# Where a streamed product turns its sums: three edits to a two-network transformer kernel

## The reference, cut to what matters

```
m = silu(c) @ mod_w + mod_b                       # both conditions, both layers
x = x + 0.5 * g0 * ffn1(norm(x) * (1 + sc0) + sh0)   # d_ff 2816, silu gated
x = x + g1 * mixer(norm(x) * (1 + sc1) + sh1)
x = x + 0.5 * g2 * ffn2(norm(x) * (1 + sc2) + sh2)
# first mixer: [latent attention, 8 heads | conv of width 31, then layer norm over 512 channels, silu] @ w_out
# second transformer: partial rope by cos/sin of positions * freq on 16 of 64 dimensions
```

## Time and profile before

| | |
|---|---|
| median of three runs | 3402.97 us |
| the profiled execution's own time | 3398.24 us |
| its span, first to last instruction | 3396.5 us |
| granted TensorE clock, mean | 0.976 |
| TensorE busy | 95% |
| weight loads of TensorE busy | 84% |
| VectorE busy | 60% |
| ScalarE busy | 42% |
| HBM read over the span | 140 GB/s |

### The profile page before, as it was taken

One profiled execution on the slowest core, in us unless ns is written; L12 is line 12 of the kernel. 1 busy time (PEld: TensorE's weight loads), 2 busy tenths in 40 slices (PEclk: granted clock), 3 DMA queues, 4 the chain that ended last, 5 costly groups with the idle time before them and its releaser, 6 DMA issues. The chain is left out here.

```text
span 3396.5 us, 51226 instructions
## 1 busy us (share of the span) xinstructions
PE 3223.1 (95%) x20294; PEld 2865.6 (84%) x20294; DVE 2026.9 (60%) x2665; ACT 1428.2 (42%) x2342; POOL 181.8 (5%) x151
## 2 busy tenths in 40 slices
PE   5999999889999999999889999999999999999998
PEld 4878777468787788877579999899999999999998
DVE  4776759747777633335445566556466665654665
ACT  3333334633333322224454444445454544454543
POOL 1000011000000100020000000300000002100000
PEclk8999999989999999999999999999999999999999
DMA  7566632026666333332136656553556665543664
GB/s 226 156 180 180 172 95 78 13 69 177 176 188 183 101 87 108 88 101 87 50 86 170 178 165 181 157 173 100 148 160 187 177 185 153 166 132 109 177 180 130
DMA packets 769421, 478.28 MB, mean 141 GB/s; under 512 B 37973, under 2 KB 746165, under 8 KB 769093
## 3 DMA queue, kind: packets, MB, share of 16 engines
q1 hardware_dynamic: 767200, 474.88, 49.3%
q10 hardware_dynamic: 2020, 0.64, 0.1%
HBM read 474.40 MB, written 1.05 MB: 140 GB/s over the span
## 5 line engine op out<-in xcount | busy, mean ns | idle before, releaser
L537 PE MATMUL psum<-normed,weights_part 128*128 128x256 f32 (+1 forms) x7392 | 1311.0, 338 | 32.0 <-DVE normed L867 11.6
L537 PEld LDWEIGHTS psum<-normed,weights_part 128*128 128x128 f32 x7392 | 1140.7, 192 | 186.9 <-issue 35.7
L523 DVE TENSOR_TENSOR weights_part<-weights,weights_part 128x2048 fp32r<-128x2048 f32 (+1 forms) x413 | 884.9, 2143 | 365.1 <-ACT weights_part L515 364.8
L515 ACT ACTIVATE weights_part<-weights 128x2048 fp32r<-128x2048 f32 (+1 forms) x413 | 739.1, 1792 | 811.1 <-PE psum L537 418.7
L537 PE MATMUL psum<-hidden,weights_part 128*128 128x256 f32 (+1 forms) x4224 | 680.4, 323 | 0.0
L537 PEld LDWEIGHTS psum<-hidden,weights_part 128*128 128x128 f32 x4224 | 614.5, 191 | 61.2
L537 PE MATMUL psum<-unscaled,weights_part 128*128 128x256 f32 x4224 | 515.3, 285 | 8.9 <-DVE unscaled L675 6.8
L537 PEld LDWEIGHTS psum<-unscaled,weights_part 128*128 128x128 f32 x4224 | 511.2, 193 | 11.4 <-DVE unscaled L675 8.6
L1086 DVE SCALAR_TENSOR_TENSOR stage<-weights,cond,stage 128x768 f32<-128x768 f32 x294 | 281.0, 1018 | 0.0
L406 POOL TENSOR_TENSOR square<-square,rinvs 128x256 f32<-128x256 f32 (+1 forms) x39 | 57.2, 1467 | 2773.6 <-ACT rinvs L391 2772.1
L880 DVE TENSOR_TENSOR rinvs<-rinvs,psum 128x256 f32<-128x256 f32 (+1 forms) x88 | 45.8, 520 | 163.2 <-ACT rinvs L774 163.2
(11 more groups left out here) (445 smaller groups left out, 2650.6 us busy)
## 6 DMA issues: line engine op xcount, KB each, us to landing
weights<-in_l_ffn_w_in SPq DMA_DIRECT2D x176, 512.0 KB, 5.1
weights<-in_ffn_w_gu SPq DMA_DIRECT2D x176, 512.0 KB, 5.0
weights<-in_l_mod_w SPq DMA_DIRECT2D x168, 384.0 KB, 3.4
weights<-in_w_in SPq DMA_DIRECT2D x34, 1024.0 KB, 5.2
weights<-in_w_gate SPq DMA_DIRECT2D x64, 512.0 KB, 5.2
weights<-in_l_ffn_w_out SPq DMA_DIRECT2D x64, 384.0 KB, 4.1
weights<-in_ffn_w_down SPq DMA_DIRECT2D x64, 384.0 KB, 3.9
weights<-in_l_ffn_w_out SPq DMA_DIRECT2D x64, 320.0 KB, 3.3
```

The costliest lines, as they stand in the source:

```text
L515: k.nc.scalar.activation(k.parts[part][0][:, W], k.slots[slot][:, W], ACT.Copy).then_inc(k.high_done, 1)
L523: k.nc.vector.tensor_tensor(k.parts[part][1][:, W], k.slots[slot][:, W], k.parts[part][0][:, W].bitcast(F32), ALU.subtract).then_inc(k.spl ...
L537: mm = k.nc.tensor.matmul(to, left[a], right[b], start=first and n == 0, stop=last and n == len(PASSES) - 1)
```

## The change

Three parts. (1) `ModStream.turn` is called inside unit u: in a wide unit between its two tiles, in a narrow one between the fifth and sixth of its eleven chunks. (2) The rope tables become a class whose load stays where it was, while the angles and the sines come after the fifth wide unit (`BETWEEN`); the loops of VectorE and ScalarE over the eleven units are so cut into five and six, which `each_unit` writes out straight. (3) In the first mixer the reciprocal is done in four pieces of 128 columns in slots 23 to 26, the scaling goes to slots 29 to 32, and silu to slots 33 and 34 (two chunks each). Only one output unit is split early, in halves: high at s=25 and 26, low at s=27 and 28; the second is left to `add_product_of_parts`, which splits what isn't `ready` behind its eight chunks of `mixed_part`.

```
                     for tile, kc in tiles:
                         if first_unit and tile == 0:
                             pe.wait_ge(t["normed"].sem, t["normed"].base + kc + 1)
+                        if stream is not None and (tile, kc) == (1, 0):
+                            stream.turn(pe, at(spec, c))
                         mm = product_of_parts(...)
                     mm.then_inc(k.unit_done, 1)
-                    if stream is not None:
-                        stream.turn(pe, at(spec, c))
...
                     for kc in range(KH):
+                        if stream is not None and kc == KH // 2:
+                            stream.turn(pe, at(spec, c))
                         mm = product_of_parts(...)
                     mm.then_inc(k.unit_done, 1)
-                    if stream is not None:
-                        stream.turn(pe, at(spec, c))
...
-            between(act)
+            if between is not None:
+                between.load(act)
...
-                each_unit(act, 0, spec.n, unit_in if s % 2 == 0 else unit_out, looped(s))
+                begun = 0
+                if s == 0 and between is not None:
+                    each_unit(act, 0, BETWEEN, unit_in, looped(s))
+                    between.tables(act)
+                    begun = BETWEEN
+                each_unit(act, begun, spec.n, unit_in if s % 2 == 0 else unit_out, looped(s))
# the same on VectorE, with between.angles(dve)
...
-CONV_MEAN, CONV_VARIANCE, CONV_SCALED = 17, 22, 23
-HEAD_AHEAD = {28: 0, 31: 1}
+CONV_MEAN, CONV_VARIANCE, CONV_ROOT, CONV_SCALED = 17, 22, 23, 28
+OUT_HIGH, OUT_LOW = (25, 26), (27, 28)
...
-    k.ahead[out.name] = 2
+    k.ahead[out.name] = 1
...
+                if s in OUT_HIGH:
+                    half = out_halves[OUT_HIGH.index(s)]
+                    last = nc.scalar.activation(out_part[0][:, half], out_slot[:, half], ACT.Copy)
...
-                    for c in ((0,), (1, 2), (3,), (), ())[s - N_HEAD_JOBS]:
+                    for c in ((), (0, 1), (2, 3), (), ())[s - N_HEAD_JOBS]:
...
+                if s in OUT_LOW:
+                    half = out_halves[OUT_LOW.index(s)]
+                    last = nc.vector.tensor_tensor(out_part[1][:, half], out_slot[:, half], out_part[0][:, half].bitcast(F32), ALU.subtract)
...
-                if s == CONV_SCALED:
+                if CONV_ROOT <= s < CONV_ROOT + 4:
+                    piece = conv_inverse[:, (s - CONV_ROOT) * P:(s - CONV_ROOT + 1) * P]
                     dve.wait_ge(t["conv_root"].sem, t["conv_root"].base + 1)
-                    nc.vector.reciprocal(conv_inverse, conv_inverse).then_inc(t["conv_inverse"].sem, 1)
+                    nc.vector.reciprocal(piece, piece).then_inc(t["conv_inverse"].sem, 1)
```

## The result

The changed kernel takes 3498.3 us in the median of four runs (3492.8 to 3505.1), the kernel before 3403.3 (3398.1 to 3403.9). The ratio is 1.0284, with a 95% interval of 1.0258 to 1.0309. The forecast was 3481 with a range of 3450 to 3520. The profiled execution of the changed kernel took 3493.37 us, its span is 3491.6, which is 95.1 more than before.

What follows compares the result with a forecast made beforehand. TensorE, busy 95% of the span, was taken as the bound. Turns +77, clock +15, tables -1 and mixer -11 gave +80 on 3398.2, so 3478; the forecast was set at 3481, range 3450 to 3520 us.

Steps and rivals of the forecast that it cites:

- The mechanism of part 1: Streamed feed-forwards: each moved turn still waits for the same VectorE accumulations, now mid-unit; new waits sum to 99 us.
- 6.3 + 1.9n - 5.5: TensorE's wait in a wide unit, n being the place of the group's last step in its hook: 2.7, 4.6, 6.4 us.
- The old 22.3 us: TensorE's 11 existing waits ahead of turns, contained in the new 99 us and not paid twice: +77 us.
- The clock: TensorE runs slower after long idle stretches: ten of thirteen waits followed by a slow stretch of 1.5 us each, +15 us.
- VectorE's waits for the turn would fall under 10 us: Streams: VectorE's next group waits for the turn 12 times, 34.1 us in all, and that mostly goes.
- Part 2: Feed-forward with the tables: the 2.8 us wait ahead of TensorE's fourth unit goes, a later one comes; net -1 us.
- wait 2.2: Tables' feed-forward: ninth unit's low part ready at 1810.8, TensorE wants it at 1808.6, so it waits 2.2 us.
- Part 3: First mixer: three TensorE waits shrink to 0.8 us left of the first, -8.5; with 2.5 of slow matmuls, -11 us.
- The long fall of the clock: Rival: the clock falls for long after most waits, +60 us for the clock, 3523 us in all; chance 0.07.
- VectorE's catching up: Rival: VectorE, no longer held by turns, ends later accumulations earlier, up to 34 us off the new waits; 3437, chance 0.06.
- the free middle: Rival: accumulations are done by mid-unit, so turns cost TensorE nothing and the 22.3 us go; 3364 us, chance 0.04.
- The sum: Whole kernel: +77 + 15 - 1 - 11 = +80 us on the profiled execution's 3398.2, giving 3478.

Runs made afterwards that it cites:

- The dose experiment: The changed kernel with the turns at three quarters of a unit instead of the middle: 3438.5 us in the median of two, ratio 1.0105.
- the placed turns: The changed kernel with each turn put where its own accumulations are over, as read from the traces: 3358.6 us, ratio 0.9872 to the kernel before.
- the kernel with part 1 alone: The kernel before with only the two calls of `turn` moved, tables and mixer as before: 3513.1 us against 3402.1, ratio 1.0332.
- the last experiment: The changed kernel with turns back behind the units and a one-column square root put ahead of the tables' absolute value: 3392.7 us, ratio 0.9972.
- The filled kernel: The changed kernel with 7 to 28 unused repeat matmuls issued ahead of each turn to keep TensorE busy: 3460.3 us, ratio 1.0168.

## Why the prediction was right, step by step

- **The mechanism of part 1**: right. The wait was named by its place, its releaser and its law, 6.3 + 1.9n - 5.5, taken as 2.9, 4.7 and 6.5 us. Measured 2.96 to 3.16, 4.65 to 4.73 and 6.42 to 6.59. Narrow units: 5.4, 1.6, 5.9 and 3.9 taken; 5.44, 1.65, 5.89 and 4.53 measured. Sum 99 forecast, 100.5 measured. The dose experiment and the placed turns show that it is the cause and not a companion.
- **The old 22.3 us are inside the new waits**: right. +77 forecast, +78.2 measured (100.5 less 22.3).
- **The clock**: right in kind, half in size, and the one term that carried the miss of 17 us. I took ten stretches at 1.5 us; the term measured 33. The count was already wrong on paper: I wrote thirteen waits between 3.9 and 6.5 us, and the list of part 1 has fifteen (six of 6.5, four of 4.7, two each of 5.4 and 5.9, one of 3.9). All fifteen were followed by a slow turn, and so were two of the four of about 3 us. Seventeen of the 21 turns took between 2.40 and 2.82 us, also those behind waits of only 2.96 and 3.16; and each cost about 33 / 17 = 1.9 us: some 21 us are the longer turns themselves, and 12 the matmuls behind them, since the slow stretch went on. The rule of the Trainium skill that was weighed ("TensorE: Matmul & The Clock Gate", "HAM oscillation") agrees in the single turn, 2.82 us for 1.53; over seventeen turns of 2.82 us it would give 24 us, an estimate that leaves out what was slow behind the turns.
- **VectorE's waits for the turn would fall under 10 us**: wrong. They are 30.5, from 34.1. VectorE asks for the turn at once after the last step, and the turn can't be sooner than that step; it still pays the transposes, at the low clock. With the waits filled and the clock up they are 20.3. It had no price for TensorE, so the sum did not feel it.
- **Part 2**: the wait of 2.81 us went, as forecast. The step that failed is "wait 2.2" at the ninth unit. It took over the 8.1 us of the earlier trace rows with two table loads of 1.28 us in them, which the kernel before paid because a square root was the last function ahead of the sines; behind silu the sines needed none, nor did silu behind them, and the low part was ready at 1907.24 for a unit that starts at 1867.06 + 7 x 5.93 = 1908.6. Forecast -1; the stage is 5.2 us shorter. By the windows of the stage, 2.3 of that is idle time (the 2.81 went, and the wait before it grew from 1.52 to 2.07), and 3.0 is matmul time (203.99 to 200.99) at a mean clock of 0.98 instead of 0.96; that part was not forecast and is luck. In three other profiles with this edit the stage took 206.7 to 208.6 us, and 211.7 in the kernel with part 1 alone. The trace of the last experiment agrees with the Trainium skill's table load ("ScalarE: Activation LUTs", "What ACT_TABLE_LOAD costs") in the 1.28 us, and shows no drain behind it: silu starts at 1806.22, 1.30 us after its load began at 1804.92.
- **Part 3**: -11 forecast (8.5 of waits, 2.5 of clock), -12.0 measured: 8.9 of idle time and 3.0 of matmul time. In five other profiles with the same mixer the stage took 258.4 to 262.4 us, against 271.4 before and 270.3 with part 1 alone, so it is worth 8 to 13. 0.8 us was to be left of the first wait, 0.67 is. The waits at the splits are gone. One wait came that I had given no price, 1.89 us ahead of the last weighing (728.97), for the copy behind the silus of s = 33. The second output unit's split stayed hidden.
- **The long fall of the clock, VectorE's catching up, and the free middle**: none came. The filled kernel prices the whole clock at 32 us, where the first of these rivals needed 60, and the new waits sum to what was worked out, where the second needed 34 us less.
- **The sum**: the profiled execution took 3493.4 where the sum gave 3478. The clock is 18 us over its term, the waits 1; part 2 came out 4 lower and part 3 one lower, which hid a quarter of the miss.

## What to carry to other kernels

Before a consumer is moved forward in an in-order queue, find what raises its semaphore and when: a wait that is moved ahead of half a unit's work can cost all of that half unit, however short it was at the old place. Here 0.97 us became 6.42, and turns that had no wait at all got 1.65 to 4.73. A unit's bookkeeping on another engine starts only when the unit before is done, so "half way through this unit" may be before the bookkeeping has begun. Where the ends of the producer differ from case to case in a fixed pattern, read them out of the trace and give each its own place: that took the same two calls from +111 us to -25 by their stages.

## What was not expected of the hardware

The wait of 2.96 us at 878.29 was followed by a slow turn and the equal one at 1114.69 was not. A slow stretch could cost as much behind the turn as in it: 34.23 us for the 144 matmuls at 841.11, against 32.91 before, beside 2.82 for 1.53 us in the turn. Matmuls that nobody reads, issued into the waits, gave back 38 of the 95 us by the medians.

```profile
1114.69 1.53 PE L1121 MATMUL psum<-consts,stage 128*128 128x128 f32 x12 [2.96 <-DVE stage L1099]
```
